# A four-layer hybrid decoder step: the order of reads, loads and weight splits around layer 1's attention and in every output product

## The reference, cut to what matters

```python
x = x + rms_norm(mixer(rms_norm(x, norm_pre)), norm_post)      # each layer
# A: u, v, g = split(h @ w_in);  v = layer_norm(gelu(v));  mixed = w_s @ v + b_s
#    out = (gelu(u) * mixed * silu(g)) @ w_out                 # w_out: 2048 x 1024
# B: q, k, v, g = split(h @ w_in);  q, k = rope(q), rope(k)
#    scores = q k' / 8 over a window of 128 keys, softmax with a sink, o = p v
#    sample tokens attend to 128 cached keys and values of their own
#    out = (o * silu(g)) @ w_out                               # w_out: 1024 x 1024
# C: a convolution, two gates, a recurrence over time; out = (hs * silu(g)) @ w_out
```

## Time and profile before

| | |
|---|---|
| median of 3 executions | 2450.81 us |
| profiled execution: time, span | 2452.49 us, 2450.7 us |
| mean granted clock of TensorE | 0.986 of full |
| PE busy | 2365.9 us, 97% |
| DVE busy | 1221.8 us, 50% |
| ACT busy | 885.5 us, 36% |
| DMA | 145.79 MB, 59 GB/s on average |

### The profile page before, as it was taken

The page is one execution under the profiler, slowest core; times in us unless marked ns, Lnnn a source line. Parts: engine busy times, 40 slices in busy tenths (PEclk is TensorE's granted clock), DMA queues, the critical chain, the costliest instruction groups (busy, mean ns, idle before and its releaser), DMA issues.

```text
span 2450.7 us, 34821 instructions
## 1 busy us (share of the span) xinstructions
PE 2365.9 (97%) x14951; PEld 2287.1 (93%) x14951; DVE 1221.8 (50%) x1741; ACT 885.5 (36%) x1254; POOL 91.5 (4%) x44
## 2 busy tenths in 40 slices
PE   8999999999999989997999989999999999999996
PEld 7999999999999878885899989999999999999996
DVE  4444454445333646665257876455444454545135
ACT  5323323223232434445353356354233223223221
POOL 0000000000000002222000001000000000000000
PEclk9999999999999989998999999999999999999998
DMA  3111111111131422111222111322111111111123
GB/s 132 45 44 44 43 44 44 44 43 36 43 96 44 160 64 53 44 50 29 98 65 90 46 35 42 117 70 88 44 52 44 36 43 44 44 44 44 44 88 104
DMA packets 58489, 145.79 MB, mean 59 GB/s; under 512 B 8904, under 2 KB 29528, under 8 KB 58328
## 3 DMA queue, kind: packets, MB, share of 16 engines
q1 hardware_dynamic: 48384, 124.78, 16.6%
q10 hardware_dynamic: 9952, 18.78, 2.5%
HBM read 121.47 MB, written 18.37 MB: 57 GB/s over the span
## 4 chain that ended last, share of the span: by engine, by line
PE 84%; DVE 8%; ACT 3%; DVEq 2%; ACTq 1%; issue 1%; DMA 1%
PE ps L491 60%; PE ps L722 5%; PE ps L515 5%; PE ps L572 3%; PE ps L635 2%; PE ps L583 2%; PE ps L628 1%; PE ps L764 1%; PE ps L739 1%; PE ps L750 1%; DVE w_lo L1324 1%; PE ps L869 1%; PE ps L775 1%; DVE l_hs L1844 1%; DVE x L1363 1%
## 5 line engine op out<-in xcount | busy, mean ns | idle before, releaser
L491 PE MATMUL ps<-l_h_hi,w_hi 128*128 128x344 f32 x2448 | 526.8, 324 | 7.9 <-DVE w_lo L1324 7.9
L491 PE MATMUL ps<-l_h_lo,w_hi 128*128 128x344 f32 x2448 | 520.5, 321 | 0.0
L491 PE MATMUL ps<-l_h_hi,w_lo 128*128 128x344 f32 x2448 | 517.4, 320 | 0.0
L491 PEld LDWEIGHTS ps<-l_h_hi,w_hi 128*128 128x128 f32 x2448 | 410.2, 188 | 9.4 <-DVE w_lo L1324 8.2
L491 PEld LDWEIGHTS ps<-l_h_lo,w_hi 128*128 128x128 f32 x2448 | 414.7, 189 | 0.0
L491 PEld LDWEIGHTS ps<-l_h_hi,w_lo 128*128 128x128 f32 x2448 | 408.6, 188 | 0.0
L1324 DVE TENSOR_TENSOR w_lo<-w_raw,w_hi 128x1024 fp32r<-128x1024 f32 x182 | 229.8, 1263 | 260.9 <-ACT w_hi L906 249.6
L906 ACT ACTIVATE w_hi<-w_raw 128x1024 fp32r<-128x1024 f32 x182 | 190.6, 1047 | 101.9 <-DMA w_raw<-in_wu 59.8
L1431 DVE TENSOR_TENSOR l_tmp<-ps,rx 128x1032 f32<-128x1032 f32 x64 | 78.9, 1233 | 287.5 <-PE ps L491 287.3
L491 PE MATMUL ps<-l_y_lo,w_hi 128*128 128x344 f32 x912 | 193.5, 320 | 0.0
L491 PE MATMUL ps<-l_y_hi,w_hi 128*128 128x344 f32 x804 | 171.3, 321 | 3.9 <-DVE l_y_lo L1527 2.8
(11 more groups left out here) (238 smaller groups left out, 3571.9 us busy)
## 6 DMA issues: line engine op xcount, KB each, us to landing
w_raw<-in_wu SPq DMA_DIRECT2D x182, 512.0 KB, 3.6
x_save<-x SPq DMA_DIRECT2D x9, 1376.0 KB, 5.8
x<-x_save ACTq DMA_DIRECT2D x16, 516.0 KB, 6.0
x<-in_xt ACTq DMA_DIRECT2D x8, 516.0 KB, 4.8
l_sw<-l_q ACTq DMA_DIRECT2D x32, 129.0 KB, 3.0
x<-x_save SPq DMA_DIRECT2D x8, 516.0 KB, 7.2
out_y<-x SPq DMA_DIRECT2D x6, 688.0 KB, 3.4
x<-in_xt SPq DMA_DIRECT2D x4, 688.0 KB, 10.3
```

Of the source, the lines that this page charges most:

```text
L491: mm = nc.tensor.matmul(ps[:, 3 * slot + ch, 0:CW], wt[:, w, k, :], mv[:, k, ch * CW:(ch + 1) * CW], start=(k == 0 and t == 0), stop=(k == ...
```

## The change

It is one of order and of queues; no computation is added or taken out.

- **Output units.** In `out_single`, `yssq` and A's second round `w_high` and `w_low` stand ahead of the wait for the unit's result. In A, `low_part(11)` stands ahead of the last `w_low` of the first round.
- **B's opening.** DVE reads the first q tile and does `w_low` of unit 4 ahead of k's rotation, and reads the second q tile ahead of the first one's rotation; the `w_low` of unit 5 stands ahead of the second. ACT does `w_high` of unit 4 ahead of the first q swap, which now stands behind the wait for `k_rot`.
- **First step.** PE runs the piece of step 0 ahead of `scores(1)`.
- **Last steps.** The six parts of the sample chain on PE and DVE move up by two or three steps, `out_part(0, 0)` to step 24 ahead of `values`, `out_part(0, 1)` by one step. The buffers of the sample chain now lie over cos, sin and `l_sw`, and SP loads them once all q tiles are rotated.
- **x back.** SP issues the transfers of `x_back` in A and B that ACT issued.

```diff
@@ sync
+                    if L.kind == "a" and u == L.u1 - 2 * KT + 6:
+                        sp.wait_ge(*L.y_done.at(MA))
+                        x_back(L, [k for k in range(KT) if k not in range(2, 2 + A_EARLY)])
...
+                    if L.kind == "b" and u == L.u0 + 18:
+                        sp.wait_ge(*L.rotated.at(KT))
+                        sp.dma_start(L.kc[:, :, 0:WIN], io["kcb"]).then_inc(L.at_in.sem, 16)
+                        sp.dma_start(L.vc[:], io["vct"].rearrange("b s f -> s b f")).then_inc(L.at_in.sem, 16)
+                    if L.kind == "b" and u == L.u1 - KT + 2:
+                        sp.wait_ge(*L.Hh.at(STEPS))
+                        sp.wait_ge(*L.y_lo_done.at(1))
+                        sp.wait_ge(*L.kout.at(16 * 6))
+                        x_back(L)
@@ tensor, layer_b
                 for i in range(STEPS):
+                    now = list(piece_range(i))
+                    if i == 0:
+                        piece(now[0])
                     if i + 1 < STEPS:
                         scores(i + 1)
-                    now = list(piece_range(i))
-                    for p in now[:1]:
+                    for p in now[:1] if i else []:
                         piece(p)
+                    if i == 24:
+                        pe.wait_ge(w_lo_done, u + 19)
+                        pe.wait_ge(*L.piece_read.at(36))
+                        pe.wait_ge(*L.Lo.at(19))
+                        out_part(0, 0, range(0, 6))
                     if i:
                         values(i - 1)
                     for p in now[1:]:
                         piece(p)
+                    if i == 23:
+                        sample_scores()
                     if i == 25:
-                        pe.wait_ge(w_lo_done, u + 19)
-                        pe.wait_ge(*L.piece_read.at(36))
-                        pe.wait_ge(*L.Lo.at(24))
-                        out_part(0, 0, range(0, 6))
+                        sample_turns()
                     if i == 26:
-                        sample_scores()
+                        pe.wait_ge(*L.Lo.at(22))
+                        out_part(0, 1, range(0, 6))
                     if i == 27:
-                        out_part(0, 1, range(0, 6))
-                    if i == 28:
-                        sample_turns()
-                    if i == 30:
                         sample_values()
@@ scalar
             def out_single(L, r):
                 for m in range(LAST):
+                    w_high(L.u1 - KT + m + 2)
                     act.wait_ge(result, 3 * (r + m + 1))
...
-                    w_high(L.u1 - KT + m + 2)
@@ scalar, layer_b
-                q_swap(2, 0)
                 w_high(L.u0 + 4)
                 act.wait_ge(*L.k_rot.at(1))
+                q_swap(2, 0)
@@ vector, layer_a
-                out_low(5, KT)
-                for m in range(KT + A_EARLY, 2 * KT):
+                out_low(5, KT - 1)
+                low_part(KT + A_EARLY)
+                out_low(KT - 1, KT)
+                for m in range(KT + A_EARLY + 1, 2 * KT):
                     low_part(m)
                 r += 2 * MA + KT
                 for m in range(LAST):
+                    w_low(L.u1 - KT + m + 2)
                     dve.wait_ge(result, 3 * (r + m + 1))
...
-                    w_low(L.u1 - KT + m + 2)
@@ vector, layer_b
+                read_q(0)
+                w_low(L.u0 + 4)
+                dve.wait_ge(*L.rope_in.at(16 * 2))
                 V.memset(L.kd[:, :, 0:P], 0.0)
                 V.memset(L.vtok[:, 0, :], 0.0)
                 rotate(L.kf[:], 64)
                 V.drain().then_inc(L.k_rot.sem, 1)
...
+                read_q(1)
+                rotate_q(0)
+                w_low(L.u0 + 5)
+                rotate_q(1)
...
-                    if i == 24:
+                    if i == 21:
                         sample_keys()
-                    if i == 26:
+                    if i == 23:
                         sample_maxima()
-                    if i == 27:
+                    if i == 24:
                         sample_normals()
-                    if i == 29:
+                    if i == 26:
                         sample_probs()
-                    if i == 31:
+                    if i == 28:
                         sample_outputs()
```

More of the change, by code:

```diff
@@ L410, in layer_loads, with x_back @@
                     sp.dma_start(L.h0[:], io["h0"]).then_inc(L.c_in.sem, 16)
-            def x_back(L):
-                for k in range(KT):
+            def x_back(L, tiles=range(KT)):
+                for k in tiles:
                     sp.dma_start(x[:, k, :], L.saved[k]).then_inc(L.x_back.sem, 16)
@@ L1112, in layer_a @@
                     high_part(m)
-                own = range(2, 2 + A_EARLY)
-                x_back(L, [k for k in range(KT) if k not in own])
                 act.dma_start(io["av"][L.j], v_new[:]).then_inc(L.vout.sem, 16)
                 for m in range(LAST):
+                    w_high(L.u1 - KT + m + 2)
                     act.wait_ge(*L.acc_done.at(m + 1))
```

42 lines of the change are left out of this document (15 added, 27 removed).

## The result

The changed kernel takes 2426.12 us (median of 4 executions, 2424.72 to 2429.86) against 2451.26 us for the kernel before on the same chip (median of 4, 2450.53 to 2452.45): ratio 0.990, 95% interval 0.9886 to 0.9914. In a second set it took 2428.07 us (4 executions, 2425.82 to 2431.79) against 2452.24. It is faster by 25.1 and 24.2 us. Executions of one kernel spread over 2 to 7 us, so most of what follows is read from stretches of profiles and not from medians.

A forecast was written before the change was run, and what follows sets the result against it. PE was taken as the bound, busy 2365.9 of 2450.7 us, so gains lie in its idle time or low clock. 2.8 + 5.8 + 2.4 + 1.5 + 8.5 = 21.0 us gave 2430; range 2423 to 2437 for 8 in 10.

The forecast's parts named there:

- the second rival: Swap lands earlier and tail runs at full clock: opening 4.6, tail 12, together 26.7 us, so 2424; chance 13%.
- A's two rounds, last pairs: A's round change and output units: PE's waits for y's split and weight rests go, 2.8 plus 5.8 us.
- x back: Transfers reading x back in A and B, moved to SP: nothing gained or lost.
- B's opening: Stop ahead of unit 4 replaced by a 6.2 us one ahead of unit 5: net 2.4 us, bounds 1.0 and 6.5.
- First step: Piece fills the wait ahead of scores(1), new 1.8 us wait ahead of turns(0): 1.5 us gained.
- Last steps: Tail of attention: keys and sample maxima move to steps where pieces fill PE; 8.5 us gained, bounds 4 and 14.
- the 3.3 added for low clock: Last steps: 3.3 us added to the full-clock end of 1171.6, giving 1174.9 against 1183.42.
- The walk: Last steps' chain followed at full clock: maxima(25) at 1123.6, maxima(31) at 1161.6, last values at 1171.6.
- The clock taking half of the tail: Rival: low clock leaves the last steps 4 us and B's opening 1, so 2436; chance 20%.
- Both chains better: Rival: swap lands earlier and tail runs at full clock, opening 4.6, tail 12 us, so 2424; chance 13%.
- Stops that move and stay: Rival: waits come back at A's second tile, ACT's emptying or v's copy; 2440 to 2449; chance 4%.
- a clock that stays low: Rival: PE stays at 1.2 GHz from the tail's first stop until its output parts end; 35 us more, 2465; chance 3%.

The follow-up runs named there:

- e1: Changed kernel with the low and high weight parts behind the emptying work again in all layers' output units and in A; median 2437.36 us.
- f4: Kernel before with the first early output part's wait loosened from step 24 to 19, and a wait added for the second; median 2448.13 us.
- e2: Changed kernel with B's opening on DVE and ACT in the order of before; median 2432.32 us.
- e4: Changed kernel with x's tiles read back by ACT's queue again in A and B; median 2429.73 us.
- f1: Changed kernel with both early output parts at steps 25 and 27 again, the first with its strict wait; median 2437.03 us.
- g1: Changed kernel run again without any edit, as common measure; median 2428.07 us.
- g3: Changed kernel with v's copy ahead of both q rotations and weight parts of units 5 and 6 one place earlier; median 2418.09 us.
- g4: Changed kernel with SP's k and v output transfers a unit later and v's copy ahead of the rotations, weight parts earlier; median 2419.26 us.
- e3: Changed kernel with the piece of step 0 behind the scores of step 1 again; median 2429.89 us.
- g2: Changed kernel with SP's four transfers of k and v to the outputs issued one unit later; median 2428.59 us.
- f3: Changed kernel with output parts and sample steps both where they stood before, only the sample's key and value transfers still early; median 2436.17 us.
- f2: Changed kernel with the sample steps three steps later, where they stood before, output parts kept at 24 and 26; median 2433.97 us.

## Why the prediction was right, and where it was off

Forecast 2430.0 us, 21.0 us under the profiled execution's or the median's time; measured 2426.12 and 2428.07, 25.1 and 24.2 under the kernel before beside them. The sum was 3 to 4 us short, and 6.8 between the two profiled executions. The first median lies nearer to the 2424 of the second rival than to the forecast, the second nearer to the forecast; the terms, not the medians, tell which was right.

**A's two rounds, last pairs: 8.6 forecast.** Right in place and kind: the waits of the earlier trace rows are gone, and e1 brings them back to a tenth of a microsecond. The stretches give 3.08 and 3.11 for the A layers, 2.40 for B's output units and 0.87 at the end, 9.5 in all; layer 0's 3.08 is its two stops of 1.39 and 0.3 of low clock. Layer C adds up to 2.5: its stretch is 362.9 to 363.0 in the three profiles with weight parts behind (before, e1, f4), and 360.2 to 362.2 in the others. 1.1 of this is its wait at the last pair (one of the four in the earlier trace rows). Most of the rest is one wait for a weight rest in its loop, up to 2.7 us before and 1.0 after; e2, e4 and f1 have it at 2.7 to 2.8 too, with their weight parts ahead, so it isn't shown to be this edit's. With the 1.1 the part is worth 10.6, by e1's median 9.3. So the term was 1 to 2 us too small: it had the stops and left out the low clock behind them.

**x back: nothing.** Right (e4).

**B's opening: 2.4 forecast, 1.5 to 1.9 measured.** The mechanism was right, the stop of 7.93 us replaced by one for v's copy, forecast at 6.2 us and found at 5.76 and, in g1, 7.2. The swap's last transfer took 6.95 us, by the row's own time of 7.07, which I kept. It landed at 867.52, which in the clock of the kernel before (whose opening starts 4.36 us later) is 871.9, against 870.7 forecast. Issued together with the outputs (both from 858.74) the swap took the same as 1.45 us behind their first (859.34 and 860.79 before; their last was issued at 860.92, so the two overlapped then too, which I had missed). The Trainium skill ("DMA: Bandwidth & Descriptors", Queues, rings and completion order) has a DMA engine take turns between its queues packet by packet; my estimate from it, a landing at 868.5, didn't come about, and no run here shows the turns themselves. The timeline of PE behind the stop:

```profile
881.28 0.37 PE L720 MATMUL ps<-ident,l_vf 128*8 128x128 f32 x1 [5.76 <-DVEq L1612]
881.38 1.20 PE L502 MATMUL ps<-l_h_hi,w_hi 128*128 128x344 f32 x3
882.38 1.06 PE L502 MATMUL ps<-l_h_lo,w_hi 128*128 128x344 f32 x3
...
884.76 0.64 PE L502 MATMUL ps<-l_h_lo,w_hi 128*128 128x344 f32 x3
885.24 0.63 PE L502 MATMUL ps<-l_h_hi,w_lo 128*128 128x344 f32 x3
```

The twelve matmuls from 881.38 to 884.76 take 3.38 us, and at the pace behind them (0.48 for three) they would take 1.9: 1.5 us were lost to the clock, where I had 2.0. What I didn't count, and what makes up the 1.2 us by which the landing was late, lies at the start of the opening, behind a stop of 1.84 us at the sums that no edit touches. The first 10 us there, in the changed kernel and in g1:

```profile
815.39:825.39 10.00, 9.99 (x43) 0.83 0.40 143
```

```profile
816.09:826.09 10.00, 10.00 (x52) 1.00 0.40 143
```

Nine matmuls fewer in the first, or 1.4 us; g3 and g4, alike but for this and the outputs, are 1.6 us apart. Of the fourteen profiles of this study five show 0.83 there (the changed kernel, e3, e4, g2, g3) and nine 1.00. g1 kept its clock there and had the longer stop ahead of unit 5 instead, and its opening comes out the same (82.94); f3, with a stop of 6.0 and the clock kept, has the shortest, 81.22.

**First step: 1.5 forecast, 1.8 measured.** The wait for POOL came as worked out, 1.9 against 1.8 us. PE kept its full clock there (1.00 against 0.89), where I had put the gain at 2 us with the clock kept and 1 without. In f2, where it fell, the gain is 0.2: the lower case was set too high, and that ten of eleven profiles kept the clock is why the term came out.

**Last steps: 8.5 forecast, 11.7 measured.** This is the step that was off, and it is one term: "the 3.3 added for low clock". The walk itself was right to half a microsecond. The last piece's end is 8.1 us earlier after than before (1110.16 against 1118.26), so the walk's times less 8.1 are 1115.5 for maxima(25), 1153.5 for maxima(31) and 1163.5 for the last values. Timeline of DVE, maxima(25) and maxima(31):

```profile
1115.25 0.48 DVE L1645 CUSTOM_DVE_ANT_0 l_sc<-ps,l_mask,l_sink 128x256 f32<-128x256 f32 x1 [0.16 <-issue]
...
1153.53 0.47 DVE L1645 CUSTOM_DVE_ANT_0 l_sc<-ps,l_mask,l_sink 128x256 f32<-128x256 f32 x1
```

and the window from the last piece's end to the last values, beside the earlier trace rows:

```profile
1110.16:1163.61 53.45, 41.79 (x288) 0.90 0.04 11
```

53.45 us, as the walk at full clock had it (1171.6 less 1118.26 is 53.3), and 56.6 with the term. PE did run at low clock, 0.90 in the mean, but not on the path: while its values, turns and scores run at low clock from 1123.39 to 1130.6, the chain that ended last lies on DVE (the sample's normals, then maxima) and ACT, and comes back to PE at 1131.82; from 1148.90 to 1159.39, with the second spell in it, it is the same. That is luck in part. In the nine profiles whose last steps are as in the changed kernel (with it, e1 to e4 and g1 to g4) they take 77.54 to 80.93 us, 78.7 on average; the full term is reached in one. e4 shows a spell that lies on the path. Its PE after 1150 us, and then that of the changed kernel:

```profile
1152.30 2.08 PE L742 MATMUL ps<-l_kd,l_q 64*128 64x256 f32 x8
```

```profile
1151.11 1.14 PE L750 MATMUL ps<-l_kd,l_q 64*128 64x256 f32 x8
```

These are the last scores, twice as long in e4, and there they are on the chain that ended last. A second spell lies on its last output matmuls and turns, where the changed kernel has none; windows of e4, then of the changed kernel:

```profile
1160.00:1165.00 5.00, 4.84 (x25) 0.66 0.00 2
```

```profile
1160.00:1165.00 5.00, 4.83 (x36) 1.00 0.00 0
```

e4's last steps take 1.8 us more. So the term should have been some 1.2 with 0 and 3.4 as its bounds. The sign that I had given, 56 to 57 us for this stretch, failed with it.

**Which part of the tail gave it.** The prediction named two causes, the wait for the cached keys and the sample's work between the maxima. Both were there, but in f3 early transfers alone give 2.4 (86.82 against 89.25, one profile each, so within the scatter; DVE's stop of 2.45 us for the cached keys in the earlier trace rows is gone in it), f4 shows that the needlessly strict wait, which I took as a result of the late keys, costs 3.6 by itself, and f1 that moving the sample's work gives next to nothing as long as the out part stands at step 25 with the strict wait. The forecast of the whole was near because I walked all the edits together; a sum over them one at a time (2.4, 0.7 and 3.0) would have missed half.

**The rivals.** The clock taking half of the tail: no, though single executions come 3.4 us near it. Both chains better: the tail did (11.7 against 12 there), though at a clock of 0.90 and not at full clock, and the opening didn't. Stops that move and stay, and a clock that stays low: not seen.

## What to carry to other kernels

When a stop is removed by reordering, look at what stands behind the moved chain and ask whether it depends on it: here one 1.23 us copy stood behind two rotations that it didn't need, and moving it, with two weight parts, gave 7.6 to 9.2 us in its stretch (10.0 by medians), against 1.5 to 1.9 for the reordering that was made. Fill holes on the pacing engine first, and walk a chain with all edits in it, since edits in one chain don't add (0.7 and 3.0 us apart, 9.2 together). Read the number in a wait against what the instruction behind it really reads: one such number was worth 4.2 us.

## What the runs showed of the hardware

- A swap's transfer of 129 KB lands in 2.4 us when nothing else is under way (g2), and the last of its four in 6.93 (e4) to 8.49 us (e3) when 1.1 MB of output transfers is issued beside it from another queue. Issued some 2 us behind those, the swap is slow to issue: 2.87 us for the second of the four instead of 0.61 (g2); 4 us behind them the four took 3.79 us instead of 2.44 (g4).
- The granted clock's spells fall at slightly different places in executions of the same code. Behind a stop of 1.84 us the clock fell in five profiles of fourteen (0.83 over 10 us) and stayed at 1.00 in nine. Over profiles of the same order the opening moves by up to 4 us (81.22 to 85.17, by the clock and by when the swap lands) and the last steps by 3.4, which is most of the spread of the executions here. In g3 and g4, with no stop in the opening, its clock is 0.98 and 1.00 instead of 0.92 to 0.96.
